# Two routed expert layers: an extra buffer for expert weights, the rank products moved, and the last down projections loaded in halves

## The reference, cut to what matters

```python
def hier_moe(h, w_group, b_group, w_expert, b_expert, w_gate, w_up, w_down):
    ...
    g_w, g_idx = lax.top_k(p_group, 1)
    ...
    e_w, e_idx = lax.top_k(jax.nn.softmax(e_logits, axis=-1), TOP_K)
    weights = g_w * (e_w / jnp.sum(e_w, axis=-1, keepdims=True))
    ...
    def body(e, acc):
        hid = jax.nn.silu(t @ w_gate[e]) * (t @ w_up[e])
        return acc + combine[:, e, None] * (hid @ w_down[e])
    out = lax.fori_loop(0, N_EXPERTS, body, jnp.zeros_like(t))
```

## Time and profile before

| what | value |
|---|---|
| median of 3 runs | 1591.61 us (1590.93 to 1596.47) |
| the profiled execution's own time | 1589.79 us |
| its span | 1588.1 us |
| TensorE busy | 1348.2 us, 85% |
| VectorE busy | 609.3 us, 38% |
| ScalarE busy | 265.7 us, 17% |
| data moved by the DMA engines | 512.98 MB, mean 323 GB/s |
| mean granted TensorE clock | 0.933 of full speed |

### The profile page before, as it was taken

How to read it: one execution, slowest core, us unless ns; L and a number is a source line. 1 busy time by engine, 2 the same in 40 slices (tenths; PEclk the granted TensorE clock), 3 DMA queues, 4 the chain that set the end, 5 groups by cost and what they waited for, 6 DMA issues and landing times.

```text
span 1588.1 us, 24085 instructions
## 1 busy us (share of the span) xinstructions
PE 1348.2 (85%) x9264; PEld 819.6 (52%) x9264; DVE 609.3 (38%) x1504; ACT 265.7 (17%) x736; POOL 104.8 (7%) x191
## 2 busy tenths in 40 slices
PE   9979998776776777989998767767777999999997
PEld 4445655443343343556564433433434875988843
DVE  3755533221132222862633212221213443677721
ACT  2134211010010011362111100100001043111100
POOL 1312000000000001211000000000001051000000
PEclk9989999898898898999999989888899999999999
DMA  8876599999999999829699999999999951544300
GB/s 302 310 294 231 215 421 420 421 421 421 422 422 422 422 422 403 304 89 411 282 421 420 420 420 420 421 420 421 421 421 380 375 174 62 196 154 159 132 0 27
DMA packets 117190, 512.98 MB, mean 323 GB/s; under 512 B 11872, under 2 KB 46620, under 8 KB 64872
## 3 DMA queue, kind: packets, MB, share of 16 engines
q1 hardware_dynamic: 115376, 507.49, 80.2%
q0 software_dynamic: 1552, 4.06, 0.8%
q10 hardware_dynamic: 168, 0.09, 0.0%
HBM read 510.54 MB, written 1.07 MB: 322 GB/s over the span
## 4 chain that ended last, share of the span: by engine, by line
PE 35%; DMA 14%; SPq 6%; DVE 1%; issue 1%; ACT 1%; POOL 0%; ACTq 0%; POOLq 0%; DVEq 0%
PE bank L2282 10%; DMA ring<-in_moe_w_up 7%; DMA BC<-in_moe_w_up 5%; SPq L1689 5%; PE bank L2313 5%; PE bank L1282 4%; PE bank L2028 3%; PE bank L537 2%; DMA ring<-in_moe_w_down 2%; PE bank L429 2%; PE bank L441 2%; PE bank L1269 1%; PE bank L1297 1%; PE bank L682 1%; PE bank L1310 1%
## 5 line engine op out<-in xcount | busy, mean ns | idle before, releaser
L1282 PE MATMUL bank<-ring,hT 128*32 128x256 f32 (+1 forms) x2976 | 307.7, 457 | 147.2 <-DMA ring<-in_moe_w_up 56.1
L1282 PEld LDWEIGHTS bank<-ring,hT 128*32 128x32 f32 (+1 forms) x2976 | 161.1, 133 | 257.3 <-issue 182.1
L1282 PE MATMUL bank<-BC,hT 128*32 128x256 f32 x1056 | 155.4, 472 | 52.6 <-DMA ring<-in_moe_w_up 31.5
L1538 DVE TENSOR_SCALAR pT<-pT 128x256 f32<-128x256 f32 x34 | 10.0, 294 | 455.9 <-ACT pT L1656 455.9
L2282 PE MATMUL bank<-hT,ring 128*128 128x256 f32 (+1 forms) x768 | 152.9, 362 | 0.0
L2282 PEld LDWEIGHTS bank<-hT,ring 128*128 128x128 f32 x768 | 135.9, 190 | 16.5
L1269 PE MATMUL bank<-A,hn 128*128 128x128 f32 x1088 | 127.2, 275 | 0.1
L1297 PE MATMUL bank<-ring,gtab 128*32 128x512 f32 (+1 forms) x768 | 123.6, 595 | 1.3 <-DMA ring<-in_moe_w_down 0.8
L1269 PEld LDWEIGHTS bank<-A,hn 128*128 128x128 f32 x1088 | 124.5, 192 | 0.2
L537 PE MATMUL bank<-ring,hT 128*128 128x512 f32 (+4 forms) x352 | 120.3, 502 | 0.5 <-DVE hT L308 0.2
L1282 PEld LDWEIGHTS bank<-BC,hT 128*32 128x32 f32 x1056 | 72.4, 135 | 92.4 <-issue 55.5
(11 more groups left out here) (307 smaller groups left out, 1528.5 us busy)
## 6 DMA issues: line engine op xcount, KB each, us to landing
ring<-in_moe_w_up SPq DMA_DIRECT2D x98, 1024.0 KB, 26.6
ring<-in_moe_w_down SPq DMA_DIRECT2D x96, 1024.0 KB, 26.4
ring<-in_moe_w_gate SPq DMA_DIRECT2D x88, 1024.0 KB, 25.5
BC<-in_moe_w_gate SPq DMA_DIRECT2D x40, 1024.0 KB, 24.2
BC<-in_moe_w_down SPq DMA_DIRECT2D x32, 1024.0 KB, 27.1
BC<-in_moe_w_up SPq DMA_DIRECT2D x26, 1024.0 KB, 26.0
ring<-in_w_ada SPq DMA_DIRECT2D x24, 1024.0 KB, 12.9
ring<-in_w_up SPq DMA_DIRECT2D x22, 1024.0 KB, 5.4
```

The source lines that it names most:

```text
L1282: i = nc.tensor.matmul(GATE[q * cap:(q + 1) * cap, part * FF:(part + 1) * FF], xg[:, c, q * cap:(q + 1) * cap], u[:, c, :], start=(c == 0) ...
```

## The change

It does six things, in both routed layers.

1. Gathers 1 to 16 read X itself, by a view with a step of eight elements, and their one-hots are multiplied by the root of the norm on VectorE (one more instruction for each block, so eight counted steps in place of seven). Gather(0) still reads the copy in `hn`.
2. `hn` becomes the 20th slot. It takes unit 19, whose load waits for gather(0). Unit 20 now waits for unit 0, and so on to unit 35; from unit 36 on the distance is 16 as before.
3. The rank products move from behind gather(0) to behind block 0's gates.
4. In block 16, six products of 512 columns go ahead of the gates and nine ahead of the ups (`keep_warm`, into bank 7), whose results nobody reads.
5. The last four downs of a layer are loaded as eight halves, the left columns of all four first. TensorE waits for the left ones before the left downs, for the right ones between, and VectorE copies the left rows as soon as the left downs are done.
6. The last `share_out` no longer waits for ScalarE's right rows; the second share product does.

Two pairs of semaphores are shared, to make room for the new ones.

```diff
-AT_ONCE = RING + EXTRA
+AT_ONCE = RING + EXTRA + 1
...
-            first = [RING + 2, RING + 3, RING, RING + 1] + from_ring[0:11] + [RING + 4, RING + 5, RING + 6, from_ring[11]]
-            again = first[0:15] + first[18:]
+            first = [RING + 2, RING + 3, RING, RING + 1] + from_ring[0:11] + [RING + 4, RING + 5, RING + 6, from_ring[11], RING + 7]
+            again = first[0:15] + [first[18]]
...
             s -= RING
+            if s == EXTRA:
+                return hn[:, :, :].rearrange("p t d -> p (t d)")
...
-            VSTEPS = 7
-            vstep = shared("block_step", VSTEPS * BLOCKS - 2)
+            VSTEPS = 8
+            vstep = shared("block_step", VSTEPS * BLOCKS - 3)
...
+            first_halves, left_down = shared("first_halves", 16 * QUAD.experts), shared("left_down", 1)
...
+            x_by_channel = X[:, :, :].rearrange("p t (j c) -> p t c j", c=DC)
             tokens_by_channel = hn[:, :, :].rearrange("p t (c j) -> p t c j", c=DC)
...
-                def gather(b):
+                def gather(b, tokens=x_by_channel):
...
                     pe.wait_ge(*rows_v(b + 1))
-                    pe.wait_ge(*rows_a(b + 1))
+                    if b < BLOCKS - 1:
+                        pe.wait_ge(*rows_a(b + 1))
...
+                def spread_ranks():
+
+                    pe.wait_ge(*ranked(1))
+                    nc.tensor.matmul(RANKS[0:32, 0:E], own_no[0:E, :].broadcast_to([E, 32]), ranks[:, 64:128],
+                                     start=True, stop=True)
+                    for k in range(2):
+                        i = nc.tensor.matmul(RANKS[:, (k + 1) * E:(k + 2) * E], ranks[:, 140 + k:141 + k].broadcast_to([E, P]),
+                                             ident[0:E, 0:E], start=True, stop=True)
+                    i.then_inc(rank_spread.sem, 1)
...
                     for part in range(2):
+                        if following is None:
+                            keep_warm(pe, 7, NB, (6, 9)[part])
                         for q in range(n):
                             here(u0 + part * n + q)
                         next(g).then_inc(unit_done.sem, n)
+                        if i is None and b == 0 and part == 0:
+                            spread_ranks()
...
-                    for q in range(n):
-                        here(u0 + 2 * n + q)
                     g = down(kind.cap, [slot(u0 + 2 * n + q) for q in range(n)])
-                    next(g)
                     if following is not None:
+                        for q in range(n):
+                            here(u0 + 2 * n + q)
+                        next(g)
                         pe.wait_ge(*tokens_a(b + 2))
+                    else:
+                        pe.wait_ge(*first_halves(16 * n))
+                        next(g).then_inc(left_down.sem, 1)
+                        for q in range(n):
+                            here(u0 + 2 * n + q)
                     next(g).then_inc(unit_done.sem, n)
...
-                gather(0)
-                pe.wait_ge(*ranked(1))
...
+                gather(0, tokens_by_channel)
...
             def product(pe, tt, nb):
 
+                if tt == 0 and nb == 1:
+                    pe.wait_ge(*rows_a(BLOCKS))
...
-                    return i
+                    wait(i)
+                    return nc.vector.tensor_tensor(hot[:, :, 0:wide], hot[:, :, 0:wide],
+                                                   nrm.rstd.unsqueeze(2).broadcast_to([P, TT, wide]), ALU.mult)
...
-                    dve.wait_ge(*after_down(m, kind))
+                    dve.wait_ge(*(after_down(m, kind) if following is not None else left_down(1)))
...
+                def last_halves(m, place):
+                    n = QUAD.experts
+                    numbers = [sp.value_load(order_i[0:1, place + q:place + q + 1], min_val=0, max_val=E - 1) for q in range(n)]
+                    load_block(m, QUAD, numbers, (0, 1))
+                    for half in range(2):
+                        for q in range(n):
+                            s, earlier = units[base + m + 2 * n + q][2], units[base + m + 2 * n + q][4]
+                            if half == 0:
+                                sp.wait_ge(*earlier)
+                            src = down_w[bass.ds(numbers[q], 1), :, :].rearrange("e (p c) n -> p (e c) n", p=P)
+                            dst = slot(base + m + 2 * n + q).rearrange("p (c n) -> p c n", c=2)
+                            sp.dma_start(dst[:, :, half * NB:(half + 1) * NB], src[:, :, half * NB:(half + 1) * NB]
+                                         ).then_inc((unit_full[s] if half else first_halves).sem, 16)
...
-                for m in range(18, 24):
+                load_fixed(18)
+                sp.wait_ge(*gathered(2))
+                for m in range(19, 24):
                     load_fixed(m)
...
-                ordered_block(3 * E - 12, QUAD, SORTED - 4)
+                last_halves(3 * E - 12, SORTED - 4)
```

More of the change, by code:

```diff
@@ L186, in build @@
         loaded = sem("loaded")
-        unit_full = [sem(f"unit_full{i}") for i in range(RING + EXTRA)]
+        unit_full = [sem(f"unit_full{i}") for i in range(AT_ONCE)]
         unit_done = sem("unit_done")
@@ L205, in build @@
         units = []
-        cursor, filled, held = [0], [0] * (RING + EXTRA), [None] * (RING + EXTRA)
+        cursor, filled, held = [0], [0] * AT_ONCE, [None] * AT_ONCE
         multiplied = []
@@ L886, in build @@
         x_in = [sem(f"x_in{tt}") for tt in range(TT)]
-        cleared, first_half_in = sem("cleared"), sem("first_half_in")
+        cleared, first_half_in = shared("cleared", 1), sem("first_half_in")
         w_in = t["diff_w_in"][0]
@@ L971, in rotate @@
             dv.done(nc.vector.tensor_tensor(t1, t1, t2, ALU.add))
-        p1_qk = sem("p1_qk")
+        p1_qk = shared("qk_out", 1)
         def rope_vector(dve):
@@ L1268, in gather @@
                         for tt in range(TT):
-                            i = nc.tensor.matmul(TOKENS[c // 4][:, c % 4 * P:(c % 4 + 1) * P], tokens_by_channel[:, tt, c, :],
+                            i = nc.tensor.matmul(TOKENS[c // 4][:, c % 4 * P:(c % 4 + 1) * P], tokens[:, tt, c, :],
                                                  hot[:, tt, :], start=(tt == 0), stop=(tt == TT - 1))
@@ L1353, in tensor @@
                     pe.wait_ge(*hn_ready(tt + 1))
-                gather(0)
-                pe.wait_ge(*ranked(1))
-                nc.tensor.matmul(RANKS[0:32, 0:E], own_no[0:E, :].broadcast_to([E, 32]), ranks[:, 64:128], start=True, stop=True)
-                for k in range(2):
-                    i = nc.tensor.matmul(RANKS[:, (k + 1) * E:(k + 2) * E], ranks[:, 140 + k:141 + k].broadcast_to([E, P]),
-                                         ident[0:E, 0:E], start=True, stop=True)
-                i.then_inc(rank_spread.sem, 1)
+                gather(0, tokens_by_channel)
                 first_blocks(block)
@@ L1378, in tensor @@
                                 for tt in range(TT):
-                                    i = nc.tensor.matmul(SIDE[0][:, c * CAP:(c + 1) * CAP], tokens_by_channel[:, tt, c, :],
+                                    i = nc.tensor.matmul(SIDE[0][:, c * CAP:(c + 1) * CAP], x_by_channel[:, tt, c, :],
                                                          hot[:, tt, 0:CAP], start=(tt == 0), stop=(tt == TT - 1))
@@ L1780, in copy_a @@
             return nc.scalar.activation(hn[:, tt, n * NB:n * NB + ps.shape[1]], ps, ACT.Copy, scale=n2.rstd[:, tt:tt + 1])
-        pe_zeroed = sem("pe_zeroed")
+        pe_zeroed = shared("cleared", 1)
         a_sq, a_rs = shared("sum_sq", 4), shared("sum_rs", 2)
@@ L1838, in build @@
         l_sq, l_ss, l_rs = shared("head_sq", 16), shared("head_ss", 16), shared("head_rs", 16)
-        l_pe, l_qk = sem("l_pe"), sem("l_qk")
+        l_pe, l_qk = sem("l_pe"), shared("qk_out", 16)
         l_items = [(x[:, tt, 2 * n:2 * n + 2, :], qk, tt) for qk, x in enumerate((q_l, k_l))
```

## The result

The changed kernel takes 1619.87 us (median of 4 runs, 1618.73 to 1620.32), the kernel before 1591.27 (4 runs, 1589.89 to 1596.47): 1.0172 times the time, 95% interval 1.0154 to 1.019, 28.6 us slower by the medians. I had predicted 1588.1 and no measurable difference. The profiled execution took 1618.73, its span is 1617.0. The number is that of a rival to which I gave 0.03, "loads from X take twice": 1618.8.

A forecast was written before the change was run, and what follows sets the result against it. The prediction took weight loads at 420 to 422 GB/s to bound the routed layers. Gains of 2.5 us in the first and 1.05 in the second, 3.5 in all, took 1591.6 to 1588.1 us, range 1583.5 to 1593.5.

The forecast's parts named there:

- loads from X take twice: Rival for gathers 1 to 16: each takes 3.65 us more, 12.9 and 14.3 lost by layer, 1618.8 us; chance 0.03.
- What bounds the kernel now: Both routed layers: weight loads at 420 to 422 GB/s set the time; gains carry through to the end.
- Start of a layer: Around block 0: unit 19 issued earlier gains 2.5 us of stream, earlier gates 0.7, together 3.2 per layer.
- the lag of 3.17: TensorE's wait for block 0's hidden rows before L1289, forecast at some 3.3 us against 1.62 before.
- cost is nothing, with thin cover: Later ranks put TensorE 2.9 us late after block 0; queued loads cover it, with 2.6 and 2.9 left.
- Gathers from X: Gathers 1 to 16 on TensorE: reading X in steps of eight elements was taken to cost nothing.
- End of a layer: Block 16 to share products: with the stream, exponential 2.4 and 0.65 us earlier; downs' wait 0.3, early copy 0.1; halves hidden.
- Sum: Both routed layers: 2.5 us gained in the first and 1.05 in the second, 3.5 in all, giving 1588.1.

The follow-up runs named there:

- x_gathers_only: Kernel before the change with only gathers 1 to 16 reading X in steps of eight and one-hots scaled, 19 slots: 1605.95 us, ratio 1.0079.
- unit_step: Changed kernel with X read in steps of one element, leaving out the channel reordering, so its result is not the layer's: 1586.56 us, ratio 0.9966.
- gathers_from_copy: Changed kernel with all gathers from the copy in hn, 19 slots, no root in the one-hots: 1590.49 us, ratio 0.9993.
- after_ranks_first: Changed kernel with the rank products back behind gather(0), ahead of block 0's gates: 1613.61 us, ratio 1.0136.
- the probe: Kernel before the change plus 64 products per layer reading X in steps of 1, 2, 4 and 8; weight loads took 192, 197, 330 and 335 ns.
- x_as_slot: Changed kernel gathering from hn, with X as the 20th slot, written back by ScalarE in block 1: 1588.33 us, ratio 0.9971.
- x_as_slot_no_warm: Changed kernel gathering from hn, with X as the 20th slot and without the fifteen extra products: 1584.39 us, ratio 0.9948.

## Why the prediction was wrong

**What bounds the kernel now** held for the kernel before, and lost stream time was the layer's time: x_gathers_only ran dry for 8.1 us in the first layer and lost 7.5 in it. From one layer to the next nothing was won or lost, 137.1 to 137.3 us in every profile; the tail varies by its clock.

**Start of a layer** held in its events (unit 19 at 179.19, the lag of 3.17). Of its gain of 3.2 a layer, 2.5 were the 20th slot's. With the slot as the main difference, unit_step against gathers_from_copy (which also has no root in its one-hots), it is 3.9 for both layers, and 4.6 without the extra products, where 5.0 was the count; the runs of each of these kernels spread over 5 to 7 us, so that is no contradiction. The prediction's "cost is nothing, with thin cover" was right about the cover and should have been carried into the next step: after_ranks_first shows 6.3 us for it once the gathers are slow.

**Gathers from X** is the step that failed. I put its cost at nothing because the transposes of X at L289 load in 191 ns. A transpose and a product read the same bytes in the same step, and only the product loses time by it: 335 against 192 ns a load, 4.06 us a gather. Two signs spoke against my row: ScalarE's copy in that step, 2171 ns against 1057, and the rule of the Trainium skill that I named beside it. A row of the same engine and access but another kind of instruction was given all the weight, and the rival 0.03. A comparison inside the row's own kind was missing: was 191 ns the free price of a transpose or the paid one? The trace of before could have told. At L399 it has transposes of the same size that read `hn` with a step of one:

```profile
L399 PEld LDWEIGHTS bank<-konst,hn x48: 138/140/230, 119.0 to 1335.6; 128*128 128x128 f32 x48
```

They load in 140 ns, as the probe's do, so L289's 191 was already a price paid for the step. It would have been a third sign against "nothing".

The rival's sum of 12.9 and 14.3 a layer meets the measured 14.6 and 15.5, but not all by its terms. It had the stream 8.5 late behind 252 us (11.7 dry, less the start's 3.2), where 14.0 were dry; it had nothing for the early copy, which gave back 0.9 and 1.0; and it had the last gather's 3.65 on the path. Without the extra products that gather is absorbed, as x_gathers_only shows, and it is the products that put it on the path. That the total came out at 1618.8 is in part luck.

**End of a layer.** The products took 5.42 and 7.99 as said. What they cost with fast gathers, where I had 3.35, stays open: the medians of the three pairs say 0.1, 0.8 and 3.9 (x_as_slot against x_as_slot_no_warm), the layers in the profiles 4.4, 5.0 and 0.3. With slow ones it was 10.5. The halves are hidden, as predicted: the downs of block 16 wait for ScalarE (0.47), not for a load. The early copy of the left rows was mis-sized: I took 0.1 out of 0 to 0.8, and from downs to share products it is 3.58 in the changed kernel, 4.50 before, 3.57 and 4.56 in the second layer, 1.9 in all. The branch and the reading of the overflow did not fill that time. My own rows had said so: they put TensorE's idle 0.86 and 0.92 ahead of the share products down to VectorE's copy, and I went by the wait at L1305 instead.

**Sum.** With a step of one the rest of the prediction gives -3.5 and unit_step measures -4.9. That doesn't confirm the terms one by one: the early copy gave 1.7 more than counted, the products' price is open, and in its profile the layers of unit_step, from gather(0) to the first share product, take 448.4 and 451.1 us, as before; there gather(0) of the second layer alone took 5.40 for 3.81.

## What to carry to other kernels

Before an operand is read in another layout, look for the price of that step in the same kind of instruction, at both steps; a row of another kind, even on the same engine, did not bound it here. For a product on TensorE keep the inner step of its operands at one or two float32: at four and eight, a load of 128 x 128 went from 192 to 330 and 335 ns here. Slack that several parts of a change each find "just enough" is to be charged once, in order: the later ranks, the longer gathers and the added products draw on the same waits and the same queued loads, and together the parts cost at least 15 us more than their sum.

## What the hardware showed that I had not expected

- The price of a step comes with a break between two and four elements (197, 330 ns), and holds for the moving stream too (275, 412 ns); transposes take 140 ns to load at a step of one and 188 at eight, and eight of them 0.88 us at either, so they lose nothing in throughput.
- A slower operand keeps the clock up. The changed kernel's mean granted clock is 0.956, that of x_gathers_only 0.95, of before 0.933: TensorE is busy where it used to wait for loads, and its time is nonetheless longer.
- The halves, loads of 0.5 MB with rows of 2 KB, landed 1.36 us apart in the full queue, 385 GB/s, where whole units run at 421: little more than their bytes.
- In some profiled executions the clock falls in the tail, 50 to 75 us behind the last share product (0.86 in that stretch), in others not: 3.5 us, as much as the whole rest of this change was to gain.
